# Expert products of a mixture-of-experts stage in plain FP32 on 32-column tiles of TensorE

## The reference, cut to what matters

```python
def moe_swiglu(h, w_router, b_router, w1, w3, w2):
    logits = (h @ w_router).astype(jnp.float32) + b_router.astype(jnp.float32)
    top_v, top_i = lax.top_k(logits, TOP_K)
    top_w = jax.nn.softmax(top_v, axis=-1)
    combine = jnp.sum(jax.nn.one_hot(top_i, N_EXPERTS, dtype=jnp.float32) * top_w[..., None],
                      axis=-2).astype(h.dtype)
    out = jnp.zeros_like(h)
    for e in range(N_EXPERTS):
        out = out + combine[..., e:e + 1] * swiglu(h, w1[e], w3[e], w2[e])
    return out
```

## Time and profile before

| | us |
|---|---|
| median of 3 runs | 1956.72 (1954.6 to 1958.21) |
| the profiled execution's own time | 1955.48 |
| its span | 1953.7 |
| PE busy | 1912.8 (98%) |
| DVE busy | 1367.3 (70%) |
| ACT busy | 985.2 (50%) |
| mean granted clock of TensorE | 0.993 of 2.4 GHz |

### The profile page before, as it was taken

The page is one execution under the profiler, slowest core; times in us unless marked ns, Lnnn a source line. Parts: engine busy times, 40 slices in busy tenths (PEclk is TensorE's granted clock), DMA queues, the critical chain, the costliest instruction groups (busy, mean ns, idle before and its releaser), DMA issues.

```text
span 1953.7 us, 23956 instructions
## 1 busy us (share of the span) xinstructions
PE 1912.8 (98%) x9306; PEld 1531.8 (78%) x9306; DVE 1367.3 (70%) x1624; ACT 985.2 (50%) x1087; POOL 102.9 (5%) x127
## 2 busy tenths in 40 slices
PE   8989999999999999999999999999999999999997
PEld 6765666668788888878788988888888888888886
DVE  4673444387767546556454578989898989898996
ACT  4424233312422122244444377777777777777775
POOL 0250000000000001004000000000000000000000
PEclk9999999999999999999999999999999999999998
DMA  9322212255355556514243299999999999999990
GB/s 376 120 86 87 76 46 95 100 183 180 108 181 186 188 168 232 184 65 141 87 151 130 98 373 355 358 349 357 350 357 350 358 349 357 349 359 349 358 350 23
DMA packets 72835, 438.21 MB, mean 224 GB/s; under 512 B 9233, under 2 KB 10001, under 8 KB 28561
## 3 DMA queue, kind: packets, MB, share of 16 engines
q1 hardware_dynamic: 61056, 393.65, 53.7%
q0 software_dynamic: 11664, 43.00, 6.8%
HBM read 435.57 MB, written 1.05 MB: 223 GB/s over the span
## 4 chain that ended last, share of the span: by engine, by line
PE 90%; DVE 5%; ACT 3%; issue 1%; DMA 1%; POOL 0%; SPq 0%; ACTq 0%; DVEq 0%; POOLq 0%
PE ps L1737 11%; PE ps L1738 11%; PE ps L1739 11%; PE ps L2189 8%; PE ps L2191 8%; PE ps L2190 8%; PE ps L2002 6%; PE ps L2203 4%; PE ps L2209 4%; PE ps L2204 4%; PE ps L1951 2%; PE ps L1910 2%; DVE wlo L1104 1%; PE ps L1977 1%; PE ps L1962 1%
## 5 line engine op out<-in xcount | busy, mean ns | idle before, releaser
L1538 DVE TENSOR_TENSOR elo<-estage,ehi 128x2048 fp32r<-128x2048 f32 x264 | 604.5, 2290 | 74.7 <-ACT ehi L982 74.0
L982 ACT ACTIVATE ehi<-estage 128x2048 fp32r<-128x2048 f32 x264 | 505.9, 1917 | 119.0 <-PE ps L2191 70.8
L1737 PE MATMUL ps<-h_hi,whi 128*128 128x512 f32 (+1 forms) x960 | 368.9, 384 | 11.4 <-DVE wlo L1104 5.6
L1739 PE MATMUL ps<-h_hi,wlo 128*128 128x512 f32 (+1 forms) x960 | 344.3, 359 | 0.0
L1738 PE MATMUL ps<-h_lo,whi 128*128 128x512 f32 (+1 forms) x960 | 344.1, 358 | 0.0
L2189 PE MATMUL ps<-ehi,xg_hi 128*128 128x512 f32 x704 | 282.8, 402 | 1.0 <-DVE elo L1538 1.0
L2191 PE MATMUL ps<-ehi,xg_lo 128*128 128x512 f32 x704 | 275.3, 391 | 0.0
L2190 PE MATMUL ps<-elo,xg_hi 128*128 128x512 f32 x704 | 275.0, 391 | 0.0
L1104 DVE TENSOR_TENSOR wlo<-stage,whi 128x2048 fp32r<-128x2048 f32 x79 | 182.7, 2312 | 93.4 <-ACT whi L713 93.4
L713 ACT ACTIVATE whi<-stage 128x2048 fp32r<-128x2048 f32 x79 | 150.9, 1910 | 163.5 <-PE ps L1739 163.4
L1737 PEld LDWEIGHTS ps<-h_hi,whi 128*128 128x128 f32 x960 | 181.1, 189 | 55.5 <-issue 17.1
(11 more groups left out here) (248 smaller groups left out, 2350.8 us busy)
## 6 DMA issues: line engine op xcount, KB each, us to landing
estage<-in_moe SPq DMA_DIRECT2D x264, 1024.0 KB, 5.0
stage<-in_split SPq DMA_DIRECT2D x79, 1024.0 KB, 5.2
gw<-in_mods POOLq DMA_DIRECT2D x80, 512.0 KB, 3.9
dw<-in_direct SPq DMA_DIRECT2D x36, 512.0 KB, 3.8
mw_a<-in_early SPq DMA_DIRECT2D x8, 512.0 KB, 8.1
mw_b<-in_early SPq DMA_DIRECT2D x8, 512.0 KB, 15.2
xT<-in_x SPq DMA_DIRECT2D x4, 512.0 KB, 5.6
gw<-in_cond_rows SPq DMA_DIRECT2D x1, 1024.0 KB, 17.7
```

Source lines behind the costliest of these rows:

```text
L982: act.activation(ehi[:, w % SPLIT, :], estage[:, w % STAGE, :], ACT.Copy).then_inc(S("e_hi_done"), 1)
L1538: dve.tensor_tensor(elo[:, w % SPLIT, :], estage[:, w % STAGE, :], ehi[:, w % SPLIT, :], ALU.subtract)\
L1737: pe.matmul(out, hi, rhs_hi, start=first, stop=False)
L1739: ins = pe.matmul(out, lo, rhs_hi, start=False, stop=last)
```

## The change

- `ehi`, `elo` and the two halves of `xg`, `ehT` go; with them go ACT's and DVE's copies. `up` and `down` wait for the landed unit itself, and the last matmul that reads a unit frees its buffer (`e_used`).
- An expert has 96 slots instead of 128: three groups of 32 tokens. If an expert had more tokens than 96, a second and a third pass would follow.
- `up` of a unit makes 4 blocks x 3 token groups x 4 tiles = 48 matmul calls: 32 stationary columns (tokens), 128 moving columns (64 of w1, 64 of w3), each tile with other weights and other output partitions.
- `down` of a unit makes 2 x 3 x 4 = 24 calls: 32 stationary columns, 256 moving ones. Three tiles take the first three quarters of the output for their own token group; the fourth takes the last quarter for each group in turn (`row_bank`, `y_d`).
- DVE multiplies (`eu`) and turns the result in 32x32 blocks (`dve.transpose`); PE's `turn` goes.
- The scatter is done at one place, into four banks; the rows of the last quarter are first copied to other partitions by DVE (`part_rows`). After the last expert the same is done, and the last squares are no longer set between the scatters.

```diff
-SPLIT = 3
+TOK = 32
-SLOTS = 128
+SLOTS = 96
+TILES_E = SLOTS // TOK
+QUADS = P // TOK
+HW = CW // QUADS
+PASSES = -(-SEQ // SLOTS)
...
+    def up_rows(cc):
+        return ps[cc % 2][:, 0:TILES_E * 2 * HW].rearrange("p (t w h) -> p t w h", t=TILES_E, w=2)
+    def row_bank(r):
+        return ps[3 + r // 2][:, r % 2 * SEQ:(r % 2 + 1) * SEQ]
...
-                sp.wait_ge(S("e_lo_done"), passed("e_lo_done", p) + v0 + (w + 1))
+                sp.wait_ge(S("e_used"), passed("e_used", p) + v0 + (w + 1))
...
-            def hi(v0, w):
-                act.wait_ge(S(f"e_in{w % STAGE}"), passed("e_in", p) + v0 * 16 + 16 * (w // STAGE + 1))
-                act.wait_ge(used, passed("e_used", p) + v0 * STAGE + (w + 1))
-                act.activation(ehi[:, w % SPLIT, :], estage[:, w % STAGE, :], ACT.Copy).then_inc(S("e_hi_done"), 1)
...
-            def lo(v0, w):
-                dve.wait_ge(S("e_hi_done"), passed("e_hi_done", p) + v0 * STAGE + (w + 1))
-                dve.tensor_tensor(elo[:, w % SPLIT, :], estage[:, w % STAGE, :], ehi[:, w % SPLIT, :], ALU.subtract)\
-                    .then_inc(S("e_lo_done"), 1)
...
+            def part_rows(e, x, used_by):
+                dve.wait_ge(S("e_used"), used_by)
+                for r in range(TILES_E):
+                    dve.tensor_copy(y_d[r * TOK:(r + 1) * TOK, :], row_bank(r)[SLOTS:P, :]).then_inc(S("y_d"), 1)
...
-                        dve.tensor_tensor(eu[:, cc % 2, :], et[:, cc % 2, :], ps[cc % 2][:, CW:2 * CW], ALU.mult).then_inc(S("eu"), 1)
+                        dve.tensor_tensor(eu[:, cc % 2, :, :], et[:, cc % 2, :, :], up_rows(cc)[:, :, 1, :], ALU.mult).then_inc(S("eu"), 1)
+                        dve.wait_ge(S("eu"), passed("eu", p) + c_ + (cc + 1))
+                        dve.transpose(ehT[:, cc % 2, :, :, :].rearrange("p t b i -> p (t b i)"), eu[:, cc % 2, :, :].rearrange("p t h -> p (t h)")).then_inc(S("ehT"), 1)
...
-            def turn(c_, pc):
-                pe.wait_ge(S("eu"), passed("eu", p) + c_ + (pc + 1))
-                for i in range(2):
-                    ins = pe.transpose(ps[2][:, pc % 2 * 256 + i * P:pc % 2 * 256 + (i + 1) * P], eu[:, pc % 2, i * P:(i + 1) * P], ident[:, :])
...
+            def landed(v0, w):
+                pe.wait_ge(S(f"e_in{w % STAGE}"), passed("e_in", p) + v0 * 16 + 16 * (w // STAGE + 1))
+                return estage[:, w % STAGE, :]
...
-            def up(cc, x, v0, w, second, between=None):
-                hi, lo = split_unit(v0, w)
+            def up(cc, x, v0, w, second):
+                rows = landed(v0, w)
                 for i in range(4):
                     kk = i + 4 * second
-                    pe.matmul(o, xg_hi[:, x % 2, kk, :], hi[:, cols], start=(kk == 0), stop=False)
-                    pe.matmul(o, xg_hi[:, x % 2, kk, :], lo[:, cols], start=False, stop=False)
-                    ins = pe.matmul(o, xg_lo[:, x % 2, kk, :], hi[:, cols], start=False, stop=(kk == KD - 1))
+                    for t in range(TILES_E):
+                        for q in range(QUADS):
+                            at = (i * QUADS + q) * 2 * HW
+                            ins = pe.matmul(ps[cc % 2][q * TOK:(q + 1) * TOK, t * 2 * HW:(t + 1) * 2 * HW], xg[:, x % 2, kk, t * TOK:(t + 1) * TOK],
+                                            rows[:, at:at + 2 * HW], start=(kk == 0 and t == 0), stop=(kk == KD - 1 and t == TILES_E - 1))
                 ins.then_inc(used, 1)
...
+                rows = landed(v0, w)
+                pe.wait_ge(S("ehT"), passed("ehT", p) + c_ + (pc + 1))
+                first, last = c == 0, c == CHUNKS - 1
+                for b in range(2):
+                    for r in range(TILES_E):
+                        for q in range(QUADS):
+                            t, part = (q, r) if q < TILES_E else (r, TILES_E)
+                            at = b * D + part * SEQ
+                            ins = pe.matmul(row_bank(r)[q * TOK:(q + 1) * TOK, :], ehT[:, pc % 2, t, b, :], rows[:, at:at + SEQ],
+                                            start=(first and b == 0 and r != 1), stop=(last and b == 1 and r != 0))
                 ins.then_inc(used, 1)
...
-SCATTER_AT = (1, 2)
+SCATTER_AT = 1
+SCATTER_BANKS = (5, 6, 2, 7)
```

More of the change, by code:

```diff
@@ L358, in build @@
     stat = fixed.take("stat", [P, 4, 4])
-    warm = fixed.take("warm", [P, 2])
+    warm = fixed.take("warm", [P, PASSES])
     zed = fixed.take("zed", [P, 2 * GROUPS])
@@ L487, in build @@
     selT = htok.take("selT", [P, 2, SEQ], F32R)
-    xg_hi = htok.take("xg_hi", [P, 2, KD, SLOTS], F32R)
-    xg_lo = htok.take("xg_lo", [P, 2, KD, SLOTS], F32R)
+    xg = htok.take("xg", [P, 2, KD, SLOTS])
+    y_d = htok.take("y_d", [P, D // QUADS])
     w_slot = htok.take("w_slot", [P, 2])
@@ L694, in _ @@
         with sp.If(most_r > SLOTS):
-            experts(1)
+            for p in range(1, PASSES):
+                experts(p)
         for name, count, k in (("out_d", 2, 2), ("out_a", 2, 0), ("out_d", 4, 6), ("out_a", 4, 4)):
@@ L1027, in expert @@
+                act.activation(y_rows[0:SLOTS, 2, 0:SEQ], row_bank(2)[0:SLOTS, :], ACT.Copy, scale=slot).then_inc(S("y_hi_e"), 1)
+                act.wait_ge(S("y_d"), passed("y_d", p) + e * 3 + 3 * x)
+                act.activation(y_rows[0:SLOTS, 3, 0:SEQ], y_d[0:SLOTS, :], ACT.Copy, scale=slot).then_inc(S("y_hi_e"), 1)
             def expert(e, v0, c_, x):
@@ L1086, in _ @@
         with act.If(most_r[0] > SLOTS):
-            last_rows_hi("fx")
-            experts(1)
-        last_rows_hi("fn")
+            for p in range(1, PASSES):
+                last_rows_hi(p, f"fx{p}")
+                experts(p)
+        last_rows_hi(1, "fn")
         for k in range(KD):
@@ L1516, in most_of_all @@
         def most_of_all():
-            step(dve.tensor_scalar(posm[:, 1, :, 0:EXPERTS], place, float(SLOTS), None, ALU.subtract))
+            for n in range(1, PASSES):
+                step(dve.tensor_scalar(posm[:, n, :, 0:EXPERTS], place, float(n * SLOTS), None, ALU.subtract))
             dve.wait_ge(S("most_full"), 1)
@@ L1653, in _ @@
         with dve.If(most_r[0] > SLOTS):
-            last_rows_lo("fx")
-            last_adds("fx")
-            experts(1)
-        last_rows_lo("fn")
+            for p in range(1, PASSES):
+                last_rows_lo(p, f"fx{p}")
+                last_adds(f"fx{p}")
+                experts(p)
+        last_rows_lo(1, "fn")
         last_adds("fn")
@@ L2192, in up @@
                 ins.then_inc(used, 1)
             def down(c_, pc, c, v0, w):
-                hi, lo = split_unit(v0, w)
-                pe.wait_ge(S("ehT_hi"), passed("ehT_hi", p) + c_ + (pc + 1))
-                for i in range(2):
-                    a_hi, a_lo = ehT_hi[:, pc % 2, i, :], ehT_lo[:, pc % 2, i, :]
-                    first, last = c == 0 and i == 0, c == CHUNKS - 1 and i == 1
-                    for f in range(2):
-                        cols = slice(i * D + f * 512, i * D + f * 512 + 512)
-                        pe.matmul(ps[3 + f][:, :], a_hi, hi[:, cols], start=first, stop=False)
-                        pe.matmul(ps[3 + f][:, :], a_hi, lo[:, cols], start=False, stop=False)
-                    if i == 0:
-                        pe.wait_ge(S("ehT_lo"), passed("ehT_lo", p) + c_ + (pc + 1))
-                    for f in range(2):
-                        cols = slice(i * D + f * 512, i * D + f * 512 + 512)
-                        ins = pe.matmul(ps[3 + f][:, :], a_lo, hi[:, cols], start=False, stop=last)
@@ L2223, in scatter @@
+                ins.then_inc(used, 1)
+            def scatter(e, x):
+                pe.wait_ge(S("y_lo_e"), passed("y_lo_e", p) + e * 3 + 3 * x)
+                pe.wait_ge(S("selT"), passed("selT", p) + e + x)
+                pe.wait_ge(S("w_slot"), passed("w_slot", p) + e + x)
+                pe.wait_ge(S("xg"), passed("xg", p) + e * 2 + (2 * x + 2))
+                for k4 in range(KD // 2):
                     for i in range(2):
                         kk = 2 * k4 + i
-                        o = ps[5 + k4 % 2][:, i * SEQ:(i + 1) * SEQ]
+                        o = ps[SCATTER_BANKS[k4]][:, i * SEQ:(i + 1) * SEQ]
@@ L2307, in _ @@
         with pe.If(most_r[0] > SLOTS):
-            last_scatter("fx")
-            experts(1)
+            for p in range(1, PASSES):
+                last_scatter(f"fx{p}")
+                experts(p)
         keep_clock(2, 6)
         last_scatter("fn")
-        for k in range(KD // 2, KD):
+        for k in range(KD):
             last_squares(k)
```

256 lines of the change are left out of this document (103 added, 153 removed).

## The result

The changed kernel takes 2026.2 us (2022.4 to 2033.6), the kernel before 1957.5: ratio 1.036, 95% interval 1.0335 to 1.0387. It is slower by 3.6%. The forecast was 1906.4, the range to 1990. The profiled execution took 2027.7 us, 2025.9 of them span.

What follows compares the result with a forecast made beforehand. PE was taken as the bound. Its expert stage was to fall from 783.8 to 733.5 us (689.0 + 36.9 + 5.1 + 2.5): 1955.5 - 50.3 = 1905.2, plus 1.2 for the median, 1906.4; range 1888 to 1990.

Steps and rivals of the forecast that it cites:

- Code itself: Loading PE's code in the expert stage: one 16 KB load per 4.1 us on average, charged nothing, 16 us at worst.
- The 3.8 us of the branch: Branch at L2307 after the expert stage, the only cold code load seen; its 3.8 us served as price per load.
- The rival: Rival 1: PE's sequencer cannot feed the tiles in the expert stage, slower from 15.1 ns per instruction; chance 0.16.
- milder form: Rival 1's mild case: code loads that come late in `up` cost part of the gain, kernel 1920 to 1945; chance 0.08.
- Pass of `up`: PE's matmul passes in the expert stage: 0.109 us for 128 columns, 0.2156 for 256; 689.0 us instead of 719.1.
- the 44.5 us for the rest of the stage: PE's expert-stage time besides `up` and `down`: 36.9 us around the experts, 5.1 for switches, 2.5 for waits.
- the 5.1 for switches: Switches of PE between narrow tiles and the whole array: 0.23 us a round trip, 22 of them, 5.1 us.
- the 2.5 for waits: Waits and starts of PE in the stage: 2.5 us kept of 8.6, as nothing in the new order waits closely.
- The end: After the stage's last product: later branch, y_d copies and a scatter without additions, net 0 us, between -2 and +3.
- rival 2: Expert loads become the bound: 777 us at 356 GB/s, kernel ends near 1932; chance 0.10.
- rival 3: Weight loads not hidden with four tiles at 128 columns: 0.134 us per pass, kernel near 2010; chance 0.04.
- rival 4: An expert with over 96 tokens needs a second and third pass of the stage, over 1,400 us more; chance 0.01.

Runs made afterwards that it cites:

- the wide `up`: Changed kernel with `up` in half as many instructions: three tiles take 384 columns per call, the fourth 128 for three token tiles; 1905.9 us, 0.975 of the kernel before.
- the small loads: Changed kernel, PE's instructions the same, but each expert load from the twelfth on brings 128 of 2048 columns (output not the reference's); 1909.8 us.
- `down` among `up`: Changed kernel with the same PE instructions reordered, the six groups of `down` between the groups of `up`; 2074.7 us, 1.060 of the kernel before.

## Why the prediction was wrong

The step that failed is the last one on instructions: "Code itself: ... If each load took that, it would just do on average, and I charge nothing, up to 16 us at worst." Measured by the wide `up` and by the small loads, code that comes late costs 122 us of the stage. What went wrong in it:

1. **An average where the worst stretch decides.** 4.1 us per piece (4.2, worked out again) is the mean over `up` and `down`. A piece that lies in `up` alone lasts 256 x 13.6 ns = 3.5 us, and a `down` later gives nothing back: a fetch starts only when PE enters the piece before, 0.4 us after it in the middle and within 1.5 in 19 of 20 beside the small loads. In the changed kernel 33 of the 46 pieces that last 3.5 us with small loads had a stop behind them, of the 46 that last 4.6 to 5 us 15, and of the 22 longer ones 1. The run that was to test this alone, `down` among `up`, bunched the loads and doesn't. On the two pieces the Trainium skill, "Advanced Engine Details and Errata", section "ISA Cache", was the better guide: it speaks of two lines, and the trace agrees, with never more than the next piece under way. The same section gives TensorE's memory as 128 KB, by its line size eight lines; no run here shows more than one piece ahead. I cited it for the size and did not draw the consequence.
2. **A quiet price for a loaded one.** The 3.8 us of the branch fell when the expert loads had ended: between 1920 and 1931.7 us all DMAs moved 1 GB/s. Beside them a piece needs 2.3 + 0.94 + 1.4 = 4.6 us in the middle and, with the 3.9 us that one wait in twenty reaches, over 6. The trace of before couldn't show it as a stop: there a piece lasts 25 us and no one waits. By these numbers it is the larger error: at 3.8 us only the 46 pieces of 3.5 would have been late, by 0.3 us each, 14 of the 104 us.
3. **The rival was priced by the wrong mechanism.** Slower was given 0.16, by the sequencer's rate with a break-even at 15.1 ns an instruction. PE took an instruction every 7.0 ns, so that mechanism is out altogether, and the late code stood beside it as a "milder form" at 1920 to 1945, 81 to 106 us too low. (Its far end is mis-added too: 60 ns an instruction gives 3472 us and not over 3,500.) The Trainium skill, "TensorE: Matmul & The Clock Gate", section "Step-by-step: what each phase is for", gives 62 ns per MATMUL where the sequencer's software decodes it; that price does not appear here, where 128 MATMULs start within 1.8 us, 14 ns each.

The other terms held. Pass of `up` 0.109 us, of `down` 0.216, exactly; stage without late code 732.4 and 731.7 against 733.5. That checks the 44.5 us for the rest of the stage only as a sum: the 5.1 for switches and the 2.5 for waits in it were not measured by themselves. The end: the stage's last product to the end of the span takes 20.2 us, before 19.4, where 0 (-2 to 3) was said; the branch at the end of the stage is as long as before, and PE starts again 2.21 us after its last product is through (1.28 before):

```profile
L2267 PEldq COMPARE_BRANCH  x1: 3749/3749/3749, 2004.1 to 2004.1; - x1
...
2007.89 1.60 PE L1780 MATMUL ps<-ident,ones 128*128 128x128 f32 x12 [2.21 <-issue]
```

**Loads as the bound** (rival 2): no, 368 GB/s run beside the wide version without a wait of PE for weights, so 356 had been the pace of the compute side. **Weight loads not hidden with four tiles** (rival 3): no, even at 64 columns. **A second pass** (rival 4): none, one stage. DVE and ACT fell further than said, to 0.42 and 0.24 us per unit where 1 was forecast, and as said that alone gave nothing.

The forecast with the missing term put in, as measured: 1905.2 + 122 = 2027; the profiled execution took 2027.7.

## What to carry to other kernels

Count instructions as well as columns. In this kernel, whose code is written out in full, each 256 of PE's instructions had to last longer than a fetch of code takes beside the kernel's own loads, 4.6 us and at times over 6, in every stretch and not on average. Tiling PE multiplies MATMULs and weight loads while it shortens each; so give each call more moving columns where the bank has room, uneven tiles included (384 for 128 here), and pay with work on an engine that is idle (here 186 us on DVE). A price read from a quiet moment of a trace is not the price beside full DMA engines.

## What the runs showed of the hardware that I had not expected

- Loads hold up an engine's code: with PE's instructions unchanged the wait before a piece's transfer is 0.4 us with loads of 25 GB/s, 1.3 with 174, 2.3 with 313, 2.6 with 293 in bunches of three, and 2.8 with rows half as long at 280.
- Loads of 64 partitions moved 216 to 233 GB/s in 1200 to 1400 us with the DMA engines full; loads of 128 had moved 424.
- Tiles with unequal calls run side by side without holding each other up: 3 x 128 columns on the fourth beside 384 on the others, PE busy 730.9 of 732.4 us.
- The granted clock was lower where PE stopped: 0.99 in the changed stage, 0.90 in `up` of 64 columns, where PE was idle 30% of the time, 1.00 in the wide version.
